# The inverse root mean square applied after the matmul: at u's eviction, and at the eviction of the first four blocks

## The reference

```
h = rms_norm(x, g_mix_pre);  proj = h @ w_in          # 1024 x 3584: recurrent group and attention group
x = x + rms_norm(concat(rec_out, attn) @ w_out, g_mix_post)
h = rms_norm(x, g_mlp_pre)
u = square(relu(h @ w_up))                            # 1024 x 4096
x = x + rms_norm(u @ w_down, g_mlp_post)
```

## Time and profile before

| | us |
|---|---|
| median of 3 runs | 1603.42 (1601.71 to 1604.54) |
| the profiled execution, its own time | 1603.46 |
| its span on the core | 1601.7 |
| mean granted TensorE clock | 0.992 |
| PE busy / DVE busy / ACT busy / POOL busy | 1554.3 / 973.5 / 833.4 / 130.2 |

### The profile page before, as it was taken

One profiled execution on the slowest core, in us unless ns is written; L12 is line 12 of the kernel. 1 busy time (PEld: TensorE's weight loads), 2 busy tenths in 40 slices (PEclk: granted clock), 3 DMA queues, 4 the chain that ended last, 5 costly groups with the idle time before them and its releaser, 6 DMA issues.

```text
span 1601.7 us, 30218 instructions
## 1 busy us (share of the span) xinstructions
PE 1554.3 (97%) x12272; PEld 1483.0 (93%) x12272; DVE 973.5 (61%) x1615; ACT 833.4 (52%) x1486; POOL 130.2 (8%) x165
## 2 busy tenths in 40 slices
PE   5999999899999999999999999998999999999996
PEld 4998889898999999999999987898899999999996
DVE  6753776774457655335888446757645675553476
ACT  6525644466455755334664365435755465551552
POOL 3120114000000000000003200230000000000000
PEclk9999999999999999999999999999999999999998
DMA  6644663352454555334544367343534555552453
GB/s 200 199 138 163 219 227 121 108 182 100 133 170 145 172 185 184 108 117 145 159 147 130 111 224 258 128 142 120 165 103 146 160 152 178 185 178 87 132 151 120
DMA packets 83237, 247.88 MB, mean 155 GB/s; under 512 B 8819, under 2 KB 26483, under 8 KB 82972
## 3 DMA queue, kind: packets, MB, share of 16 engines
q1 hardware_dynamic: 83100, 245.96, 48.4%
HBM read 234.11 MB, written 14.44 MB: 155 GB/s over the span
## 4 chain that ended last, share of the span: by engine, by line
PE 86%; DVE 8%; DMA 2%; ACT 2%; issue 1%; SPq 1%; POOL 0%; DVEq 0%; ACTq 0%
PE ps L962 67%; PE ps L959 7%; PE ps L1026 3%; DVE w_rest L1291 1%; PE ps L1177 1%; PE ps L1164 1%; DVE reg L1329 1%; PE ps L1192 1%; DMA kc<-kcT 1%; DVE x L1333 1%; DVE norm_every L1314 1%; DVE square_sum L1304 1%; DMA bias<-rel_scratch 1%; DVE s_in L1500 1%; PE ps L990 1%
## 5 line engine op out<-in xcount | busy, mean ns | idle before, releaser
L962 PE MATMUL ps<-h_high,w_rest 128*128 128x320 f32 (+1 forms) x1920 | 583.7, 304 | 9.3 <-DVE h_rest L1353 5.8
L962 PE MATMUL ps<-h_rest,w_high 128*128 128x320 f32 (+1 forms) x1920 | 571.5, 298 | 0.0
L962 PE MATMUL ps<-h_high,w_high 128*128 128x320 f32 (+1 forms) x1920 | 571.3, 298 | 0.0
L703 ACT ACTIVATE w_high<-w_raw 128x1024 fp32r<-128x1024 f32 x384 | 402.0, 1051 | 230.0 <-PE ps L962 230.0
L1291 DVE TENSOR_TENSOR w_rest<-w_raw,w_high 128x1024 fp32r<-128x1024 f32 x380 | 470.4, 1242 | 63.1 <-ACT w_high L703 63.0
L962 PEld LDWEIGHTS ps<-h_high,w_rest 128*128 128x128 f32 x1920 | 367.8, 192 | 25.9 <-issue 20.7
L962 PEld LDWEIGHTS ps<-h_rest,w_high 128*128 128x128 f32 x1920 | 368.1, 192 | 0.8 <-issue 0.4
L962 PEld LDWEIGHTS ps<-h_high,w_high 128*128 128x128 f32 x1920 | 367.7, 192 | 0.0
L962 PE MATMUL ps<-u_high,w_rest 128*128 128x320 f32 (+1 forms) x1024 | 305.3, 298 | 2.8 <-DVE u_rest L1395 2.4
L962 PE MATMUL ps<-u_high,w_high 128*128 128x320 f32 (+1 forms) x1024 | 303.1, 296 | 0.0
L962 PE MATMUL ps<-u_rest,w_high 128*128 128x320 f32 (+1 forms) x1024 | 303.1, 296 | 0.0
(11 more groups left out here) (175 smaller groups left out, 1592.8 us busy)
## 6 DMA issues: line engine op xcount, KB each, us to landing
w_raw<-w SPq DMA_DIRECT2D x384, 512.0 KB, 3.5
kc<-kcT SPq DMA_DIRECT2D x16, 512.0 KB, 8.3
vc<-vc SPq DMA_DIRECT2D x16, 512.0 KB, 6.8
s_in<-s SPq DMA_DIRECT2D x8, 512.0 KB, 6.7
ss<-s_in SPq DMA_DIRECT2D x8, 512.0 KB, 5.8
bias<-rel_scratch SPq DMA_DIRECT2D x8, 512.0 KB, 4.5
rel_scratch<-rel_row SPq DMA_DIRECT2D x1, 2560.0 KB, 12.1
bias<-rel_scratch SPq DMA_DIRECT2D x8, 256.0 KB, 5.0
```

Of the source, the lines that this page charges most:

```text
L703: A.activation(whi[:, v % RING], raw[:, v % RING], ACT.Copy).then_inc(S["w_hi"], 1)
L962: last = pe.matmul(ps[:, bank, 0:n], wt[:, slot, c, :], xt[:, c, :], **flags)
```

## The change

There are two parts.

**MLP norm.** `pre` for the MLP (k = 2) no longer multiplies by the factor: ACT makes `h_high` from `x` and the gain alone, DVE makes `h_rest` from `x`, the gain and `h_high` in one instruction, and neither waits for the norm. The factor goes to a tile of its own (`every_u`, laid over `probs_s` and `ks_tok`) and comes in at the eviction of each U block, which moves from ACT to DVE: `max(ps, 0) * factor` into `tmp` (then squared on ACT, as before). In phase IB, `norm_sum(2, 0)` moves from behind block 22 to behind block 25, and the parts of `pre` go one block earlier. For half 1 (phase U2A) the steps stay where they are.

**Start.** The first four blocks (F of half 0) multiply x * gain without the factor (`first_high` by ACT, `first_rest` by DVE), and use four banks (0, 1, 3, 4). DVE multiplies their result by the factor into `tmp`, and ACT's sigmoids read `tmp`. The first norm's sum moves behind block 1; its `pre`, with the factor as before, now feeds block 4. The weight of block 0 is loaded first of all and its rest made by DVE. The pieces of the diff stand in the order of the file: SP, POOL, ACT, PE, DVE.

```diff
-EVICT = {"F": "a", "Q": "d", "I": "a", "V": "a", "QA": "a", "K": "a", "G": "d", "O": "a", "U": "a", "D": "d"}
+FIRST_BANKS = (0, 1, 3, 4, 2)
+N_FIRST = 4
+EVICT = {"F": "a", "Q": "d", "I": "a", "V": "a", "QA": "a", "K": "a", "G": "d", "O": "a", "U": "d", "D": "d"}
...
-    put("IB", 22, "norm_sum", 2, 0)
     for p in range(5):
-        put("IB", 23 + (p + 1) // 2, "pre", 2, 0, p)
+        put("IB", 22 + (p + 1) // 2, "pre", 2, 0, p)
+    put("IB", 25, "norm_sum", 2, 0)
...
+def scaled_before(m):
+
+    l, r = divmod(max(0, m - 2), 8)
+    return 8 * (m - 2 * l - (r > 1) - (r > 3))
...
+            load(0)
             for c in range(0, KC, 2):
                 sp.dma_start(x[:, c:c + 2, 0:WIDE[0]], xT[:, c:c + 2, 0:WIDE[0]]).then_inc(S[f"x_part{c // 2}"], 16)
-            sp.dma_start(prm[:], par).then_inc(S["p_in"], 16)
-            for v in range(RING):
+                if c == 0:
+                    sp.dma_start(prm[:], par).then_inc(S["p_in"], 16)
+            for v in range(1, RING):
                 load(v)
...
-            rest(0)
+            for v in range(1, RING):
+                rest(v)
             for c in range(1, KC, 2):
                 pool.wait_ge(S["h_hi"], c + 1)
-                V.tensor_tensor(hl[0][:, c, :], acc[0][:, c, :], hh[0][:, c, :].bitcast(F32), ALU.subtract).then_inc(S["h_odd"], 1)
-            for v in range(1, RING):
-                rest(v)
+                V.tensor_tensor(hl[0][:, c, :], first_x[:, c, :], hh[0][:, c, :].bitcast(F32), ALU.subtract).then_inc(S["h_odd"], 1)
...
                 for c in (2 * p, 2 * p + 1):
-                    act.wait_ge(S["nap"], 8 * m + c + 1)
-                    A.activation(hh[h][:, c, :], acc[h][:, c, :], ACT.Copy).then_inc(S["h_hi"], 1)
+                    if k == 2:
+                        act.wait_ge(S["x_odd" if c % 2 else "x_even"], 4 * (4 * l + h) + p + 1)
+                        A.activation(hh[h][:, c, :], x[:, c, FIRST[h]:FIRST[h] + WIDE[h]], ACT.Copy, scale=gain[:, c:c + 1])\
+                            .then_inc(S["h_hi"], 1)
+                    else:
+                        act.wait_ge(S["nap"], scaled_before(m) + c + 1)
+                        A.activation(hh[h][:, c, :], (acc[h] if m else first_x)[:, c, :], ACT.Copy).then_inc(S["h_hi"], 1)
...
                 if o.kind == "F":
+                    if o.n < N_FIRST:
+                        act.wait_ge(S["f_mul"], o.n + 1)
+                        src = tmp[:, o.n, 0:n]
...
-                    if o.kind == "U":
-                        A.activation(tmp[:, s, 0:n], src, ACT.Relu).then_inc(S["ev_a"], 1)
...
-                    act.wait_ge(S["ev_a"], o.evn)
+                    act.wait_ge(S["ev_d"], o.evn)
                     if k >= 2:
                         act.wait_ge(S["u_set"], k - 1)
                     A.activation(tmp[:, 2 + k % 2, 0:n], tmp[:, s, 0:n], ACT.Square)
...
+            def x_high(p):
+                gain = prm[:, 0, 0:KC]
+                act.wait_ge(S[f"x_part{p}"], 16)
+                for c in (2 * p, 2 * p + 1):
+                    A.activation(first_h[:, c, :], x[:, c, 0:WIDE[0]], ACT.Copy, scale=gain[:, c:c + 1]).then_inc(S["x_hi"], 1)
+
             act.wait_ge(S["one_set"], 2)
+            act.wait_ge(S["p_in"], 16)
+            x_high(0)
+            high(0)
+            for p in range(1, 4):
+                x_high(p)
+            high(1)
             for p in range(4):
                 x_sq(0, 0, p)
-            high(0)
+            high(2)
+            high(3)
             norm_sum(0, 0, 0)
-            high(1)
+            act.wait_ge(S["lb_set"], 2)
+            A.activation(lb[:], lb[:], ACT.Exp).then_inc(S["lb_exp"], 1)
             for p in range(4):
                 pre(0, 0, 0, p)
-            high(2)
-            high(3)
...
-                hi, lo = (uh[h], ul[h]) if o.kind == "D" else (hh[h], hl[h])
+                hi, lo = (first_h, first_l) if o.n < N_FIRST else (uh[h], ul[h]) if o.kind == "D" else (hh[h], hl[h])
...
+                        if k == 2:
+                            V.scalar_tensor_tensor(hl[h][:, c, :], x[:, c, cols], gain[:, c:c + 1], hh[h][:, c, :].bitcast(F32),
+                                                   ALU.mult, ALU.subtract).then_inc(done, 1)
...
+            def f_scaled(o):
+                dve.wait_ge(S["blk"], o.n + 1)
+                V.tensor_tensor(tmp[:, o.n, 0:WIDE[0]], ps[:, bank_of(o), 0:WIDE[0]], every[:, 0:WIDE[0]], ALU.mult)\
+                    .then_inc(S["f_mul"], 1)
...
+                elif o.n in (2, 3):
+                    f_scaled(o)
+                elif o.kind == "U":
+                    k = n_up[0]
+                    if o.k == 0 and o.tile == 0:
+                        dve.wait_ge(S["n_inv"], norm_no(o.l, 2, o.h) + 1)
+                    if k >= 2:
+                        dve.wait_ge(S["u_sq"], k - 1)
+                    dve.wait_ge(S["blk"], o.n + 1)
+                    V.scalar_tensor_tensor(tmp[:, gate_slot[o.n], 0:n], src, 0.0, every_u[o.h][:, 0:n], ALU.max, ALU.mult)\
+                        .then_inc(S["ev_d"], 1)
...
+            x_low(0)
+            x_low(1)
+            dve.wait_ge(S["w_hi"], 1)
+            V.tensor_tensor(wlo[:, 0], raw[:, 0], whi[:, 0].bitcast(F32), ALU.subtract).then_inc(S["w_lo_0"], 1)
+            for c in range(2, KC):
+                x_low(c)
             dve.wait_ge(S["l_in"], 16)
...
+            for p in range(4):
+                x_sq(0, 0, p)
+            norm_sum(0, 0, 0)
+            dve.wait_ge(S["n_inv"], 1)
+            for o in outs[:2]:
+                f_scaled(o)
+            for p in range(5):
+                pre(0, 0, 0, p)
```

More of the change, by code:

```diff
@@ L404, in build @@
             [place(f"bias1_{s}", [P, 2, 512], offset=o) for s, o in enumerate((o_vt[0], o_f))]]
+    first_h = place("first_high", [P, KC, WIDE[0]], F32R, offset=part(0, 8))
+    first_l = place("first_rest", [P, KC, WIDE[0]], F32R, offset=part(1, 0))
+    first_x = place("first_x", [P, KC, WIDE[0]], offset=part(1, 10))
     rel_sb = place("rel_sb", [P, NREL], offset=o_key[1])
@@ L427, in build @@
     free_at = {}
-    lo_of = {v: ("w_lo_p", v + 1) for v in range(RING)}
+    lo_of = {v: ("w_lo_p", v) if v else ("w_lo_0", 1) for v in range(RING)}
     for o in outs:
@@ L713, in x_sq @@
             def x_sq(l, h, p):
-                if h == 0:
-                    act.wait_ge(S[f"x_part{p}"], 16)
-                elif p == 0:
+                if h and p == 0:
                     act.wait_ge(S["x_in1"], 16)
@@ L774, in evict @@
                     dst = (vt if o.kind == "I" else va)[o.h]
[L775 removed]
+                    A.activation(dst[0:rows, o.tile, 256 * o.k:256 * o.k + 256], ps[0:rows, bank_of(o), 0:256],
                                  ACT.Copy).then_inc(S["ev_a"], 1)
@@ L944, in gemm @@
             def gemm(o):
-                h, n, bank = o.h, WIDE[o.h], o.n % GEMM_BANKS
+                h, n, bank = o.h, WIDE[o.h], bank_of(o)
                 for v in o.loads:
@@ L1339, in pre @@
                 cols = slice(FIRST[h], FIRST[h] + n)
-                if p == 0:
+                to = acc[h] if m else first_x
+                if p == 0 and k == 0:
                     dve.wait_ge(S["n_inv"], m + 1)
-                    if m == 0:
-                        dve.wait_ge(S["p_in"], 16)
-                if p < 4:
+                if p < 4 and k == 0:
                     for c in (2 * p, 2 * p + 1):
-                        V.scalar_tensor_tensor(acc[h][:, c, :], x[:, c, cols], gain[:, c:c + 1], every[:, 0:n],
+                        V.scalar_tensor_tensor(to[:, c, :], x[:, c, cols], gain[:, c:c + 1], every[:, 0:n],
                                                ALU.mult, ALU.mult).then_inc(S["nap"], 1)
@@ L1608, in a_spr, with x_low @@
                                            ALU.mult, ALU.mult).then_inc(S["a_scaled"], 1)
-            for p in range(4):
-                x_sq(0, 0, p)
-            norm_sum(0, 0, 0)
-            for p in range(5):
-                pre(0, 0, 0, p)
+            def x_low(c):
+                dve.wait_ge(S["x_hi"], c + 1)
+                V.scalar_tensor_tensor(first_l[:, c, :], x[:, c, 0:WIDE[0]], prm[:, 0, c:c + 1], first_h[:, c, :].bitcast(F32),
+                                       ALU.mult, ALU.subtract).then_inc(S["x_lo"], 1)
+            x_low(0)
[4 more added lines that the diff above has]
+                x_low(c)
             dve.wait_ge(S["l_in"], 16)
```

75 lines of the change are left out of this document (46 added, 29 removed).

## The result

The changed kernel took 1608.06 us in the median of 22 runs (1605.40 to 1613.37), the kernel before 1604.03 us in 22 runs beside it (1600.89 to 1606.23). The ratio is 1.0028, 95% interval 1.0021 to 1.0035: slower by 0.28%, 4.0 us. Forecast were 1605.5 us, within 1598.5 to 1610.5, and "no change, a little on the slow side". The edits run later are called e1 to e11.

What follows compares the result with a forecast made beforehand. PE was taken as the bound, busy 1554.3 of 1601.7 us, leaving only waits and half-clock time to win. Start 3.2, IB -5.2 and U3B +4.1 gave +2.1 on 1603.46: 1605.5 us, range 1598.5 to 1610.5.

Steps and rivals of the forecast that it cites:

- Start, +3.2: Program start: first matmul 8 us earlier, but block 4 waits for its weight, then runs at low clock; +0.8 to +4.1.
- Rival (a): Program start: the 8 us head start is kept, giving 1594.4 us; chance 0.07.
- Phase IB, -2.6 each: Phase IB, both layers: the sum's wait gives way to a 3.05 us key wait; clock holding taken as half; -5.2 in all.
- Rival (b): Clock holds in both IB phases and the start is at its low bound: 1600.7 us; chance 0.2.
- U3B, +4.1: U3B, both layers: U's eviction on DVE makes PE wait, +1.7 in layer 0, +2.4 in layer 1; +2.5 to +5.5.
- the prediction's walk: U3B, layer 0, step by step: waits of 0.3, 1.0 and 1.6, then D3B's last chunk waits for `u_rest`; +1.7.
- Rival (c): U3B: VectorE becomes the bound and the clock falls once or twice, 3.0 each: 1608.5 to 1611.5 us; chance 0.2.
- U0A, nothing: U0A: attention leaves DVE idle 1 to 2.5 us ahead of each `u_rest`, so U's eviction there costs nothing.
- its last rival: Start at its high bound with both IB phases low: 1609.3 us; chance 0.1.

Runs made afterwards that it cites:

- e1: Changed kernel's start only, with U's eviction on ScalarE, scaled h and IB places as in the kernel before: 1606.23 us, ratio 1.0020 to the kernel before.
- e11: e8 with the factor at U's eviction in the second half too: 1592.64 us, ratio 0.9938 to the kernel before.
- e10: e8 with the changed kernel's start put in: 1592.49 us, ratio 0.9937 to the kernel before.
- e8: Kernel before's start, factor at U's eviction in first half only, post's IB parts one block apart, GpSimd's rest held: 1590.23 us, ratio 0.9923 to the kernel before.
- e6: Changed kernel with GpSimd's second rest of the second half held until U0A's fourth block is done: 1607.60 us, ratio 1.0026 to the kernel before.
- e4: Changed kernel with the fifth and sixth weights made ahead of the sigmoids: 1607.59 us, ratio 1.0029 to the kernel before.
- e7: e4 with blocks 2 and 3 scaled right behind block 5's rest and two later weight rests on GpSimd: 1608.48 us, ratio 1.0036 to the kernel before.
- e2: Kernel before's start, with both halves of U scaled at the eviction on VectorE: 1604.82 us, ratio 1.0011 to the kernel before.
- e3: Kernel before with only U's relu moved to VectorE, no factor, h scaled as before: 1607.73 us, ratio 1.0034 to the kernel before.
- e9: Kernel before with post's IB parts one block apart, third norm's sum behind block 24, pre behind 24 to 26: 1596.14 us, ratio 0.9958 to the kernel before.

## Why the prediction was right, and where it was not

The time lay inside the range, 2.6 us above the forecast, and the sign was as the prediction leaned. The loss is just large enough to be told from nothing, so the words "no change" were not right: 1608.06 lies in what the prediction called slower (over 1606.6), which had a chance of 0.36 against 0.44. That the sum came as near as it did is in part luck, since terms that were off by up to 2.5 us went both ways. Of the terms +3.2, -5.2, +4.1 and nothing:

- **Start, +3.2.** Measured +2.7, and +2.5 in e10 against e8. The chain was right to 0.6 us at each link: root at 22.3 (21.9 forecast, where it begins), the last `h_high` ended at 32.8 (32.4), block 4 at 38.5 (37.9), PE idle for 8.65 (8.7). The first matmul was late, 10.2 for 9.4. The low clock cost 1.5, not 2.6, as half of its stretch passed in the wait. That size belongs to this execution: in e6 the low level lasted until 43.8, 5.4 us of work with 20 matmuls, and cost 2.7. Rival (a) fell; e4 and e7 add that a head start cannot be kept by moving the next weights, as the wait goes on to block 6 or 7.
- **Phase IB, -2.6 each.** Measured -1.4 and -2.2. The mechanism was right: the wait goes to the key eviction, 3.05 us forecast, 3.13 measured. The size was a half chance between -1.4 and -3.85 for whether the clock holds, and it fell in both layers, for 6.8 us in the first and 3.4 in the second. Mis-sized by 1.6 us in all in this execution. By the clock of the other traces the first is the exception: e2, e4, e6 and e7 have the same wait of 3.1 us in both layers, the clock fell all eight times, and each time for 3.4 us, where it had fallen for 6.8 behind each wait of 4.3 us (before, e1, e3, both layers). Their steps from IB to V, counted as above, are -2.2 to -2.6, near the -2.6 of the forecast. So the clock did neither of the two things that the prediction weighed, hold or fall as before; it fell for half as long, and the mean of the two hit that by luck. Rival (b) rested on the page "TensorE: Matmul & The Clock Gate" of the Trainium skill (section "HAM oscillation — how this bites in real kernels"), by which the shorter gap would have been safe; the windows 319.30:325.20 and 1106.30:1109.70 at 0.53 speak against that reading. So do e9 and e10, where the clock fell behind 2.4 us, the wait that the prediction had counted among those that do not bring it down.
- **U3B, +4.1.** Measured +3.6, +1.5 in layer 0 (1.7 forecast) and +2.1 in layer 1 (2.4), the same in after, e2, e3 and e11. In layer 0 PE waited 0.3, 0.8, 1.4 and 1.5 us, where the prediction's walk had 0.3, 1.0, 1.6 and the last chunk. The clock did not fall in U3B in any trace with the eviction on DVE there. Rival (c) fell.
- **U0A, nothing.** This is the step that failed. "U0A's attention leaves DVE idle 1 to 2.5 us ahead of each `u_rest`: nothing" looked at DVE's idle time, and not at who waits behind it. The eviction put DVE between PE and ACT. ACT's squares, its weight and its table load, all ahead of the exponential, then started later (0.65 us, read in e6 against before; e3, which moves the eviction alone, has 1.0 of the growth), and `u_rest` fell under GpSimd's instruction (0.6 us, shown by e6). +1.24 in each layer by the waits, +2.5 in all.

2.7 - 3.6 + 3.6 + 2.5 + 0.3 = +5.5, as in the spans; by the forecast's terms it was +2.1. The medians differ by 4.0, as the profiled execution of after was 0.95 us above its median. Of the 3.4 us between forecast and spans, U0A is 2.5 and IB 1.6, and 0.3 lies at the sample attention; the start and U3B, each 0.5 too high, take 1.0 back. Two sums of the prediction do not come out: its last rival takes U3B at 4.5 where the term is 4.1 (1608.9, not 1609.3), and the parts of "slower" add up to 0.39, not 0.36.

What stays open: why the clock fell for 3.4 us at the sample attention in some executions and not in others, with waits of 0.8 to 1.0 us for `kc` in both, and why it fell behind U3B's 2.4 us in two of five traces. Whether DVE alone bounds the start: a run that relieves DVE without GpSimd was not made. And what the spread `post` gives by itself in the kernel before: e9 moves the third norm's sum too.
